# Turning the modulation rows of a two-block transformer in groups of four slabs instead of one by one

## The chip, the cores and the metric

The kernel runs on one core of a Trainium2 chip. The metric is the device time of one execution in microseconds (us). The engines are called as in the profile: PE is TensorE (PEld its weight loads), DVE is VectorE, ACT is ScalarE, POOL is GpSimd, SP is SyncE, which issues the weight transfers.

## What is computed

The whole program is two small networks, one after the other, on 256 tokens of width 1024. The change touches only the first one, a two-layer block that is steered by two condition vectors, `c` for the tokens of the picture and `c_ctx` for 256 context tokens. For each layer l:

```
m      = silu(c) @ w_mod[l] + b_mod[l]        # 1024 -> 6144, and the same for c_ctx
shift1, scale1, gate1, shift2, scale2, gate2 = split(m, 6)
h = h + gate1 * mixer(rmsnorm(h, norm1_g) * (1 + scale1) + shift1)
h = h + gate2 * ffn(rmsnorm(h, norm2_g) * (1 + scale2) + shift2)
```

The mixer is a projection `w_in` into eight blocks (pool, neighbourhood attention q/k/v, retention q/k/v and gate), then pooling, attention and retention, then `w_out`. All in fp32.

## The kernel before, in words

**Weights** come as a stream of slabs of up to 128 x 4096 fp32 (2 MB) through a ring of three slots. SP issues the two halves of slab n once slab n-3 has been used (`loads_sp`, L479). The order of the slabs is written out by hand in `slabs` (L173). The matrix `w_mod[l]` is cut into 12 slabs of 512 columns. Slabs 0 to 3 of layer 0 come first; slabs 4 to 11 come one behind each of the eight slabs of `w_in` of layer 0; the 12 slabs of layer 1 follow, and are used during attention (0 to 5) and retention (6 to 11) of layer 0.

**One modulation slab** takes four steps, on three engines:

1. `mod_pe` (L602): PE multiplies the slab by silu(c). The weights of the product are a 128 x 32 slice of `g.cs`, of which columns 0 and 1 hold silu(c) and silu(c_ctx) and the other 30 are zero. Eight chunks of 128 inputs are dealt over the four column groups of the array, two each, so the result is a 128 x 512 bank with two useful rows in each quarter (four partial sums).
2. `mod_act` (L634): ACT copies that bank into one of two buffers `mod_rows`.
3. `mod_sum_pe` (L620): four fp32 products of PE, each with 128 columns of `mod_rows` as weights and the first two columns of a 0/1 table as moving operand, turn the rows into columns and add the four partial sums.
4. `mod_dve` (L641): DVE adds the bias and writes 4 columns x 2 of `g.mod`; where a scale is complete, it also makes the gain (L656).

**Banks.** PSUM has eight banks. The rows of step 1 go to bank seven, in both layers. The result of step 3 goes to bank six in layer 0 and to bank seven in layer 1. So in layer 0 step 3 of slab i waits until DVE has read slab i-1, and in layer 1 step 1 of slab i+1 waits for step 4 of slab i. In layer 0 bank six also takes the attention's outputs.

**Order of the work.** Each engine's program is a list written by hand. At the start (`first_block`, L3297) PE does slab 0, its step 3, slab 1, the sum of squares of the first norm, step 3 of slab 1, then slabs 2 and 3 with their steps. In the projection (`proj_pe`, L1024) PE does, for each of the eight names, the products of `w_in`, then step 3 of the slab before, then step 1 of the next slab. ACT puts step 2 behind its copies of that name (`proj_act`, L1055), DVE puts step 4 two names later (`proj_dve`, L1089); for the name `pool` its step 4 stands behind the addition of the attention bias, L1202. In attention (`attn_mod_pe`, L1238) PE does step 1 at odd steps i and step 3 at the even step behind; DVE's step 4 is `attn_mod_dve` (L1248), in the same order; in the first four steps ACT also makes tables of powers for retention (`powers_act`, L1217). Retention (`ret_pe`, L1292) does step 1 at even i up to 10 and step 3 at i+1.

The weights of `w_in` and of `w_out` (layer 0) are split into two parts for three products in place of one (`upper_act` L521, `lower_dve` L531, `mm3` L466, with its products on L469, L470, L471). All plain fp32 products, those of the modulation among them, are on L475.

## Time and profile before

| | us |
|---|---|
| median of 3 runs | 2822.08 |
| lowest, highest | 2820.62, 2824.28 |
| span of the profiled execution | 2811.5 |
| PE busy in it | 2664.0 |
| modulation, from the first slab's product to the last slab's bias | 10.3 to 309.0 |

The execution's own time is not listed beside its profile; the span lies 10.6 us below the median, which is what lies around it. Rows give the start of an instruction in us from the start of the span, then its duration, the engine, line, operation and tiles, and in brackets how long the engine had been idle before it and what ended that. Consecutive instructions of one kind are one row ("x8"). The granted clock (PEclk) is 1.00 for TensorE's full clock and 0.50 for half of it.

### The profile page before, as it was taken

The page shows a single profiled execution, that of the slowest core. Times are in us where ns is not written, and L with a number is a line of the kernel's source. Part 1 is how long each engine was busy: PE and PEld are TensorE (multiplying, and loading weights), DVE is VectorE, ACT ScalarE, POOL GpSimd, SP SyncE. Part 2 cuts the span into 40 slices and gives each one's busy share as a digit, 9 for nine tenths or more (in the row PEclk, how much of TensorE's full clock was granted, in tenths as well). Part 3 has the DMA queues.
Part 4 walks back from the last instruction along what each step waited for, and adds up shares of the span by engine and source line. Part 5 has one row for each costly group of instructions (what it writes and reads, how often), then busy time and mean ns, then how long its engine had stood idle before and what let it go on. Part 6 is the DMA issues. An engine that isn't in the chain of part 4 may idle for free.

```text
span 2811.5 us, 38891 instructions
## 1 busy us (share of the span) xinstructions
PE 2664.0 (95%) x15416; PEld 2257.2 (80%) x15416; DVE 1820.9 (65%) x1912; ACT 1462.4 (52%) x1624; POOL 29.6 (1%) x40
## 2 busy tenths in 40 slices
PE   6999989999898999888899998899999999999998
PEld 4775678888786899777799986788888888888887
DVE  4224665543535776674355454688888889888887
ACT  3225343332325555522244444577777777777775
POOL 0002000000002000000000000000000000000000
PEclk9999999999999999998799999899999999999998
DMA  8456322222231445320044441699999999999996
GB/s 344 169 206 252 138 91 90 96 99 86 102 130 55 167 163 179 125 90 1 1 155 176 171 169 43 232 368 349 366 348 343 371 347 365 349 369 344 344 371 240
DMA packets 84359, 590.43 MB, mean 210 GB/s; under 512 B 9616, under 2 KB 10000, under 8 KB 19472
## 3 DMA queue, kind: packets, MB, share of 16 engines
q1 hardware_dynamic: 82800, 576.79, 55.0%
q10 hardware_dynamic: 1440, 11.93, 1.1%
q8 instruction: 90, 1.47, 0.2%
q14 instruction: 29, 0.24, 0.0%
HBM read 587.63 MB, written 1.05 MB: 209 GB/s over the span
## 4 chain that ended last, share of the span: by engine, by line
PE 85%; DVE 8%; ACT 4%; issue 1%; DMA 1%; DVEq 0%; POOL 0%; ACTq 0%; POOLq 0%; SPq 0%
PE banks L469 23%; PE banks L470 23%; PE banks L471 23%; PE banks L475 16%; DVE ring_rounded L531 2%; ACT ring_rounded L521 1%; PE banks L2869 1%; DMA ring<-in_stream 1%; PE banks L909 1%; DMA hT<-in_h 1%; DVE rstd L816 0%; DVE aT L2266 0%; ACT scratch L986 0%; DVE activations L1427 0%; DVE aT L832 0%
## 5 line engine op out<-in xcount | busy, mean ns | idle before, releaser
L531 DVE TENSOR_TENSOR ring_rounded<-ring,ring_rounded 128x2048 fp32r<-128x2048 f32 (+4 forms) x168 | 339.7, 2023 | 430.1 <-ACT ring_rounded L521 429.0
L470 PE MATMUL banks<-aT_rounded,ring_rounded 128*128 128x256 f32 (+1 forms) x1632 | 531.5, 326 | 0.0
L470 PE MATMUL banks<-ring_rounded,activations_rounded 128*128 128x512 f32 x1344 | 523.3, 389 | 0.0
L521 ACT ACTIVATE ring_rounded<-ring 128x2048 fp32r<-128x2048 f32 (+4 forms) x168 | 284.8, 1697 | 397.3 <-PE banks L471 381.7
L469 PE MATMUL banks<-aT_rounded,ring_rounded 128*128 128x256 f32 (+2 forms) x1120 | 339.0, 303 | 24.6 <-DVE aT_rounded L841 12.5
L470 PEld LDWEIGHTS banks<-aT_rounded,ring_rounded 128*128 128x128 f32 x1632 | 317.7, 195 | 23.8 <-issue 0.7
L471 PE MATMUL banks<-aT_rounded,ring_rounded 128*128 128x256 f32 (+2 forms) x1120 | 336.3, 300 | 0.0
L470 PEld LDWEIGHTS banks<-ring_rounded,activations_rounded 128*128 128x128 f32 x1344 | 252.7, 188 | 50.0
L3043 DVE TENSOR_TENSOR ring_rounded<-ring,aT_rounded 128x2048 fp32r<-128x2048 f32 x112 | 255.1, 2286 | 22.5 <-ACT aT_rounded L2961 21.5
L3043 DVE TENSOR_TENSOR ring_rounded<-ring,tables_rounded 128x2048 fp32r<-128x2048 f32 x112 | 254.0, 2286 | 23.5 <-ACT tables_rounded L2961 22.5
L2961 ACT ACTIVATE tables_rounded<-ring 128x2048 fp32r<-128x2048 f32 x112 | 215.0, 1920 | 85.2 <-DMA ring<-in_stream 75.3
L2961 ACT ACTIVATE aT_rounded<-ring 128x2048 fp32r<-128x2048 f32 x112 | 214.9, 1919 | 81.2 <-DMA ring<-in_stream 70.0
L469 PE MATMUL banks<-activations_rounded,ring_rounded 128*128 128x512 f32 (+1 forms) x724 | 246.6, 341 | 9.6 <-DVE aT_rounded L846 7.1
L469 PEld LDWEIGHTS banks<-aT_rounded,ring_rounded 128*128 128x128 f32 (+1 forms) x1120 | 218.7, 195 | 34.2 <-issue 18.8
L471 PE MATMUL banks<-activations_rounded,ring_rounded 128*128 128x512 f32 (+1 forms) x724 | 245.1, 339 | 0.0
L471 PEld LDWEIGHTS banks<-aT_rounded,ring_rounded 128*128 128x128 f32 (+1 forms) x1120 | 218.4, 195 | 5.7
L469 PE MATMUL banks<-tables_rounded,activations_rounded 128*128 128x512 f32 x448 | 176.5, 394 | 0.0
L469 PE MATMUL banks<-aT_rounded,activations_rounded 128*128 128x512 f32 x448 | 176.1, 393 | 0.0
L471 PE MATMUL banks<-tables_rounded,activations_rounded 128*128 128x512 f32 x448 | 174.7, 390 | 0.0
L471 PE MATMUL banks<-aT_rounded,activations_rounded 128*128 128x512 f32 x448 | 174.7, 390 | 0.0
L470 PE MATMUL banks<-activations_rounded,ring_rounded 128*128 128x256 f32 (+1 forms) x528 | 168.1, 318 | 0.0
L469 PEld LDWEIGHTS banks<-activations_rounded,ring_rounded 128*128 128x128 f32 x724 | 137.9, 190 | 26.4 <-issue 8.8
(333 smaller groups left out, 4774.3 us busy)
## 6 DMA issues: line engine op xcount, KB each, us to landing
ring<-in_stream SPq DMA_DIRECT2D x501, 1024.0 KB, 6.0
ring<-in_stream SPq DMA_DIRECT2D x32, 704.0 KB, 5.2
ring<-in_stream SPq DMA_DIRECT2D x28, 768.0 KB, 6.0
activations<-in_rpb ACTq DMA_DIRECT2D x2, 1536.0 KB, 6.2
ring<-in_stream SPq DMA_DIRECT2D x6, 512.0 KB, 5.0
tables<-in_tab_b ACTq DMA_DIRECT2D x1, 2436.0 KB, 8.8
tables<-in_tab_a ACTq DMA_DIRECT2D x1, 2304.0 KB, 13.0
hT<-in_h ACTq DMA_DIRECT2D x1, 2048.0 KB, 16.0
```

Of the source, the lines that this page charges most:

```text
L469: pe.matmul(out, exact(upper), exact(w_upper), start=start, stop=False)
L470: pe.matmul(out, exact(upper), exact(w_lower), start=False, stop=False)
L471: return pe.matmul(out, exact(lower), exact(w_upper), start=False, stop=stop)
L475: return pe.matmul(out, lhsT, rhs, start=start, stop=stop)
L521: act.activation(exact(upper), w, ACT.Copy).then_inc(g.s["act_pieces"], 1)
L531: dve.tensor_tensor(exact(w), w, rounded(upper), ALU.subtract).then_inc(g.s["dve_pieces"], 1)
L909: last = pe.transpose(ps[:, o * w + P * t:o * w + P * t + P], probs[:, j % 2, o, P * t:P * t + P], g.tab("ident"))
L2869: last = pe.transpose(g.psum[4 + q % 2][:, P * j:P * j + P], g.hb[:, q % 2, P * j:P * j + P], g.tab("ident"))
L2961: act.activation(exact(g.upper[u % UPPERS]), g.units[u % EXPERT_RING], ACT.Copy).then_inc(s["act_split"], 1)
L3043: dve.tensor_tensor(exact(w), w, rounded(g.upper[u % UPPERS]), ALU.subtract).then_inc(s["dve_split"], 1)
```

## The change

`MOD_GROUP = 4`. Four slabs share one bank: the silu(c) buffer becomes one row of 32 x 8 + 8 columns, in which the two columns of chunk k stand at 32 k + 6 and 32 k + 7. Slab j of a group takes as weights the 32 columns from 32 k + 2 (3 - j), so its two useful columns are 2j and 2j + 1 and the rest are zeros. The first product of the group starts the accumulation, the last ends it. Step 2, step 3 and step 4 come once for a group: one copy of ACT, four products of PE with eight moving columns instead of two, and two additions of DVE (one for each of the two condition vectors) on 16 columns.

```diff
+MOD_GROUP = 4
 def mod_pe(g, pe, l, i):
-    pe.wait_ge(*g.bank_free("seven"))
-    ps = g.open(("mod rows", l, i), "seven")
+    group, j = i // MOD_GROUP, i % MOD_GROUP
+    if j == 0:
+        pe.wait_ge(*g.bank_free("seven"))
+        g.open(("mod rows", l, group), "seven")
+    ps = g.psum[g.bank_of[("mod rows", l, group)]]
     for half in range(2):
         for c in range(4):
             k = 2 * c + half
-            last = mm(pe, ps[32 * c:32 * c + 32, :], g.cs[:, k, :], w[:, 512 * k:512 * k + 512], half == 0, half == 1)
+            first = 32 * k + 2 * (MOD_GROUP - 1 - j)
+            last = mm(pe, ps[32 * c:32 * c + 32, :], g.cs[:, first:first + 32], w[:, 512 * k:512 * k + 512],
+                      (j, half) == (0, 0), (j, half) == (MOD_GROUP - 1, 1))
 def mod_sum_pe(g, pe, l, group):
-    for j in range(4):
-        last = mm(pe, ps[:, 2 * j:2 * j + 2], g.mod_rows[:, i % 2, P * j:P * j + P], g.tab("mod_rows")[:, 0:2])
+    w = 2 * MOD_GROUP
+    for q in range(4):
+        last = mm(pe, ps[:, w * q:w * q + w], g.mod_rows[:, group % 2, P * q:P * q + P], g.tab("mod_rows")[:, 0:w])
 def mod_dve(g, dve, l, group):
+    for s in range(2):
+        out = g.mod[:, l, first:first + 4 * MOD_GROUP, s].rearrange("p (j q) -> p q j", j=MOD_GROUP)
+        b = g.vec[:, a:a + 4 * MOD_GROUP].rearrange("p (j q) -> p q j", j=MOD_GROUP)
+        dve.tensor_tensor(out, ps[:, :, :, s], b, ALU.add).then_inc(g.s["dve_modulation"], 1)
+def ends_group(i):
+    return i is not None and i % MOD_GROUP == MOD_GROUP - 1
 # proj_pe
-            if i > MOD_FIRST:
-                mod_sum_pe(g, pe, l, i - 1)
+            if i > MOD_FIRST and ends_group(i - 1):
+                mod_sum_pe(g, pe, l, i // MOD_GROUP - 1)
             mod_pe(g, pe, l, i)
 # attn_mod_dve
-    if l == 0 and i == 0:
-        mod_dve(g, dve, 0, 10)
     if l == 0 and i == 1:
-        mod_dve(g, dve, 0, 11)
+        mod_dve(g, dve, 0, 2)
 # first_block, ACT
+        squares_act(g, e, ("n1", 0), g.hT, T2, None)
         mod_act(g, e, 0, 0)
-        squares_act(g, e, ("n1", 0), g.hT, T2, None, then=lambda: mod_act(g, e, 0, 1))
-        for i in range(2, MOD_FIRST):
-            mod_act(g, e, 0, i)
 # first_block, PE
         mod_pe(g, e, 0, 0)
-        mod_sum_pe(g, e, 0, 0)
         mod_pe(g, e, 0, 1)
         for k in range(KD):
             sum_pe(g, e, ("n1", 0), T2, k)
-        mod_sum_pe(g, e, 0, 1)
         for i in range(2, MOD_FIRST):
             mod_pe(g, e, 0, i)
-            mod_sum_pe(g, e, 0, i)
+        mod_sum_pe(g, e, 0, 0)
```

The calls of steps 2, 3 and 4 in the projection, attention and retention are kept where a group ends and dropped elsewhere. Groups end with slabs 3, 7 and 11 of each layer: at the start, at the name `pool`, at `gate`, at attention step 7, and at retention steps 2 and 10; step 3 stands one place behind each of these (behind slab 3 at the start). DVE's first wait for the vectors stays, without its first addition.

## Rows read from the trace of the kernel before

**Rows 1.** The page: busy time by engine, share of the span, instructions.
```profile
PE 2664.0 (95%) x15416; PEld 2257.2 (80%) x15416; DVE 1820.9 (65%) x1912; ACT 1462.4 (52%) x1624; POOL 29.6 (1%) x40
```
**Rows 2.** Stretches of 20 us: length, busy by engine (instructions), PEclk, DMA share, GB/s.
```profile
100.00:120.00 20.00, 17.74 (x120) 14.35 (x119) 6.42 (x4) 5.09 (x8) 0.00 (x0) 0.83 0.66 258
...
200.00:220.00 20.00, 17.17 (x115) 10.44 (x112) 8.52 (x16) 15.09 (x34) 4.82 (x6) 0.83 0.61 240
...
260.00:280.00 20.00, 19.90 (x167) 10.74 (x166) 7.58 (x8) 8.44 (x16) 4.83 (x6) 1.00 0.83 306
280.00:300.00 20.00, 18.68 (x138) 9.05 (x137) 14.26 (x18) 9.30 (x13) 0.00 (x0) 1.00 0.77 292
```
**Rows 3.** PE's waits from 0 to 320 us: total, times, longest.
```profile
PE banks L475 <- DVE modulation L649: 5.8, 3, 2.3
...
PE banks L475 <- ACT scratch L999: 2.9, 3, 1.9
```
**Rows 4.** Line L637, step 2: duration ns min/median/max.
```profile
L637 ACT ACTIVATE mod_rows<-banks x24: 582/597/599, 14.0 to 301.8; 128x512 f32<-128x512 f32 x24
```
**Rows 5.** Timeline of PEld: step 3, then step 1, in the projection.
```profile
96.26 1.03 PEld L475 LDWEIGHTS banks<-tables,mod_rows 128*128 128x128 f32 x8
97.31 0.16 PEld L475 LDWEIGHTS banks<-ring,silu_c 128*32 128x32 f32 x8
...
99.16 0.19 PEld L469 LDWEIGHTS banks<-ring_rounded,scratch_rounded 128*128 128x128 f32 x1 [0.84 <-issue]
```
**Rows 6.** Timeline behind the products of `pool`.
```profile
112.87 0.17 DVE L649 TENSOR_TENSOR modulation<-banks,vectors 128x8 f32<-128x8 f32 x1
...
113.19 1.84 PE L475 MATMUL banks<-tables,mod_rows 128*128 128x2 f32 x8 [2.26 <-DVE modulation L649]
...
114.96 3.64 PE L475 MATMUL banks<-ring,silu_c 128*32 128x512 f32 x16
118.53 0.79 PE L469 MATMUL banks<-scratch_rounded,ring_rounded 128*128 128x512 f32 x1
...
119.87 0.39 PE L469 MATMUL banks<-scratch_rounded,ring_rounded 128*128 128x512 f32 x1
```
**Rows 7.** Line L489: second half of slab 3 with the one before, issue and landing.
```profile
L489 SPq DMA_DIRECT2D ring<-in_stream x2: 328/639/950, 14.0 to 14.4; - x2
...
DMA to landing us min/median/max: 13.4/14.4/15.5
```
**Rows 8.** Timeline of the start, slab 3.
```profile
31.43 1.92 PE L475 MATMUL banks<-ring,silu_c 128*32 128x512 f32 x16
...
33.42 0.60 ACT L637 ACTIVATE mod_rows<-banks 128x512 f32<-128x512 f32 x1 [3.03 <-PE banks L475]
...
35.16 0.17 DVE L649 TENSOR_TENSOR modulation<-banks,vectors 128x8 f32<-128x8 f32 x1 [3.46 <-PE banks L475]
```
**Rows 9.** Timeline of the first attention steps.
```profile
207.85 1.26 PE L475 MATMUL banks<-tables,mod_rows 128*128 128x2 f32 x8 [2.21 <-DVE modulation L649]
...
211.05 3.64 PE L475 MATMUL banks<-ring,silu_c 128*32 128x512 f32 x16
...
213.15 0.69 ACT L986 ACTIVATE scratch<-banks,nmax 128x512 f32<-128x512 f32 x1 [1.45 <-DVE nmax L952]
...
216.52 0.58 ACT L637 ACTIVATE mod_rows<-banks 128x512 f32<-128x512 f32 x1
...
221.48 1.01 ACT L999 ACTIVATE scratch<-banks 128x1024 f32<-128x1024 f32 x1
...
222.63 1.09 PE L475 MATMUL banks<-scratch,activations 128*64 128x128 f32 x16 [1.86 <-ACT scratch L999]
```
**Rows 10.** Timeline of the end of retention.
```profile
292.35 3.35 DVE L1427 RECIPROCAL activations<-activations 128x512 f32<-128x512 f32 x1 [1.56 <-ACT activations L1368]
...
298.63 1.92 PE L475 MATMUL banks<-ring,silu_c 128*32 128x512 f32 x16 [1.32 <-DVE modulation L649]
...
301.78 0.59 ACT L637 ACTIVATE mod_rows<-banks 128x512 f32<-128x512 f32 x1
...
302.51 1.02 PE L475 MATMUL banks<-tables,mod_rows 128*128 128x2 f32 x8 [0.90 <-ACT mod_rows L637]
```

More of the change, by code:

```diff
@@ L620, in mod_sum_pe @@
-def mod_sum_pe(g, pe, l, i):
-    if (l, i) == (0, 0):
+    if j == MOD_GROUP - 1:
+        g.also("pe_modulation", ("mm", "mod rows", l, group))
+def mod_sum_pe(g, pe, l, group):
+    if (l, group) == (0, 0):
         pe.wait_ge(g.const_in["tab_head"], 16)
-    pe.wait_ge(g.s["act_modulation"], g.at("free", ("mod rows", l, i)))
+    pe.wait_ge(g.s["act_modulation"], g.at("free", ("mod rows", l, group)))
     kind = "six" if l == 0 else "seven"
     pe.wait_ge(*g.bank_free(kind))
-    ps = g.open(("mod", l, i), kind)
-    for j in range(4):
-        last = mm(pe, ps[:, 2 * j:2 * j + 2], g.mod_rows[:, i % 2, P * j:P * j + P], g.tab("mod_rows")[:, 0:2])
+    ps = g.open(("mod", l, group), kind)
+    w = 2 * MOD_GROUP
+    for q in range(4):
+        last = mm(pe, ps[:, w * q:w * q + w], g.mod_rows[:, group % 2, P * q:P * q + P], g.tab("mod_rows")[:, 0:w])
@@ L630, in mod_sum_pe @@
     last.then_inc(g.s["pe_modulation"], 1)
-    g.count("pe_modulation", ("mm", "mod", l, i))
-def mod_act(g, act, l, i):
-    act.wait_ge(g.s["pe_modulation"], g.at("mm", "mod rows", l, i))
-    act.activation(g.mod_rows[:, i % 2, :], g.bank(("mod rows", l, i))[:, :], ACT.Copy).then_inc(g.s["act_modulation"], 1)
-    g.count("act_modulation", ("free", ("mod rows", l, i)))
-def mod_dve(g, dve, l, i):
-    if (l, i) == (0, 0):
-        dve.wait_ge(g.const_in["vec"], 16)
-    dve.wait_ge(g.s["pe_modulation"], g.at("mm", "mod", l, i))
-    a = g.vec_at["b_mod"] + 48 * l + 4 * i
-    ps = g.bank(("mod", l, i))[:, 0:8].rearrange("p (c s) -> p c s", s=2)
-    b = g.vec[:, a:a + 4].unsqueeze(2).broadcast_to((P, 4, 2))
-    dve.tensor_tensor(g.mod[:, l, 4 * i:4 * i + 4, :], ps, b, ALU.add).then_inc(g.s["dve_modulation"], 1)
-    g.count("dve_modulation", ("free", ("mod", l, i)))
+    g.count("pe_modulation", ("mm", "mod", l, group))
@@ new lines, in mod_act, with mod_dve @@
+def mod_act(g, act, l, group):
+    act.wait_ge(g.s["pe_modulation"], g.at("mm", "mod rows", l, group))
+    act.activation(g.mod_rows[:, group % 2, :], g.bank(("mod rows", l, group))[:, :], ACT.Copy).then_inc(g.s["act_modulation"], 1)
+    g.count("act_modulation", ("free", ("mod rows", l, group)))
+def mod_dve(g, dve, l, group):
+    dve.wait_ge(g.s["pe_modulation"], g.at("mm", "mod", l, group))
+    first = 4 * MOD_GROUP * group
+    a = g.vec_at["b_mod"] + 48 * l + first
+    ps = g.bank(("mod", l, group))[:, 0:8 * MOD_GROUP].rearrange("p (q j s) -> p q j s", q=4, j=MOD_GROUP)
+    for s in range(2):
+        out = g.mod[:, l, first:first + 4 * MOD_GROUP, s].rearrange("p (j q) -> p q j", j=MOD_GROUP)
+        b = g.vec[:, a:a + 4 * MOD_GROUP].rearrange("p (j q) -> p q j", j=MOD_GROUP)
+        dve.tensor_tensor(out, ps[:, :, :, s], b, ALU.add).then_inc(g.s["dve_modulation"], 1)
+        g.count("dve_modulation", ("free", ("mod", l, group)))
@@ L1344, in ret_pe @@
             mod_pe(g, pe, 1, mod_in_retention(i))
-        if l == 0 and i and mod_in_retention(i - 1) is not None:
-            mod_sum_pe(g, pe, 1, mod_in_retention(i - 1))
+        if l == 0 and i and ends_group(mod_in_retention(i - 1)):
+            mod_sum_pe(g, pe, 1, mod_in_retention(i - 1) // MOD_GROUP)
 def over_heads(g, pe, l, what, j):
@@ L1378, in ret_act @@
                 g.count("act_retention", ("free", ("ro", l, j)))
-        if l == 0 and mod_in_retention(i) is not None:
-            mod_act(g, act, 1, mod_in_retention(i))
+        if l == 0 and ends_group(mod_in_retention(i)):
+            mod_act(g, act, 1, mod_in_retention(i) // MOD_GROUP)
         if i == 0:
@@ L1445, in ret_dve @@
                 centre(j)
-        if l == 0 and i and mod_in_retention(i - 1) is not None:
-            mod_dve(g, dve, 1, mod_in_retention(i - 1))
+        if l == 0 and i and ends_group(mod_in_retention(i - 1)):
+            mod_dve(g, dve, 1, mod_in_retention(i - 1) // MOD_GROUP)
         if l == 0 and 5 <= i < 11:
@@ L3328, in first_block @@
         rstd_dve(g, e, ("n1", 0), T2)
-        for i in range(1, MOD_FIRST):
-            mod_dve(g, e, 0, i)
+        mod_dve(g, e, 0, 0)
     for l in range(2):
@@ L3426, in build @@
         g.pool_w = g.sb("pool_w", 2, 4, 64)
-        g.cs, g.mod, g.gain = g.sb("silu_c", KD, 32), g.sb("modulation", 2, 48, 2), g.sb("gain", 2, 2, KD, 2)
+        g.cs, g.mod, g.gain = g.sb("silu_c", 32 * KD + 2 * MOD_GROUP), g.sb("modulation", 2, 48, 2), g.sb("gain", 2, 2, KD, 2)
         g.cend = g.sb("chunk_ends", 4, 8)
```

34 lines of the change are left out of this document (17 added, 17 removed).

## Prediction

> **What bounds the kernel now.** I read the page first, for who is busy: PE is, 95% of the span [rows 1]. So a step taken off PE pays in full wherever PE is the one that others wait for, and a step taken off ACT or DVE pays only where PE waits for it. The modulation is over at 309 us, so I then read only the first 320 us, in stretches, for where PE is not full or not at its full clock. Between 100 and 120 us and between 200 and 220 us both are seen at once: busy 17.7 and 17.2 of 20 us, and a granted clock of 0.83 [rows 2]. The waits say why: PE waited 5.8 us in three waits for the modulation's bias addition on DVE [rows 3]. The timelines of these places give the rest.
>
> **Step 3, in the projection.** Its eight weight loads begin at 96.26 and those of the next slab at 97.31 [rows 5]; the loads before and behind run without a gap, so one step 3 costs PE 1.05 us at full clock. Eight moving columns instead of two lie behind these loads, and I cost them at nothing (bounds: nothing, and 0.3 us for each of the six, a quarter more). Step 1 itself, 97.31 to 99.16, is 1.85 us [rows 5] and keeps its number and shape. Between 60 and 195 us PE has one wait only, that of rows 6. Removed are steps 3 of slabs 4, 5, 6, 8, 9 and 10. Five of them at 1.05 are **5.3 us**; that of slab 6 is in the next part.
>
> **The wait behind `pool`.** Step 3 of slab 6 needs bank six, which DVE gives back at 113 us only, because its addition stands behind the attention bias. PE was idle 2.26 us, from 110.93 on. Then it ran at half clock: step 3 took 1.84, step 1 3.64 instead of 1.92, and the first products of the next slab come at 118.53; from 119.87 the product again takes its 0.39 [rows 6]. In the changed kernel nothing stands between the products of `pool` and slab 7: slab 7 is the last of its group and waits for no bank. Step 1 ends at 110.93 + 1.85 = 112.78, so the next products come 118.53 - 112.78 = 5.75 us earlier. The three products from 118.53 to 119.87 took 1.34 us and want 0.68. Together **6.3 us** (6.4, rounded down). What they need, the lower part of their slab, was ready before the bias addition began, so nothing else is late next.
>
> **The start.** PE loses three steps 3 and the waits for ACT's copies between slabs. But slab 3 cannot start before its second half is there: issued at 14.4 and 15.5 us to landing, 29.9 [rows 7]; it started at 31.43 [rows 8]. At full clock step 1, copy, step 3 and addition follow as before and all is 1.5 us earlier. But slab 2 now ends at about 27.5 (it starts when the squares are summed at 26, in place of 27.8), and 2.4 us of idle time open, as long as the two that were followed by half clock [rows 6, 9]. Then step 1 takes 3.64 less what ran before the fall and step 3 takes 0.8 more, about 1.9 us in all: 0.4 us later than before. A second addition on DVE is 0.1 us more. I take **0**, with -1 and +3 as bounds (the upper one if the clock also rises one step earlier in the first products).
>
> **The head of attention.** Step 3 of slab 11 waited 2.21 us for DVE's addition for slab 10, which stands behind the first maximum; then PE ran at half clock, step 1 again 3.64 [rows 9]. That wait goes: bank six was given back long before. But here PE is not what ends last. ACT makes exponentials and tables of powers in turn, 3.37 us a step (213.15 to 216.52), then a copy of rows 0.58, and PE waits for its copy of the first transposes, 221.48, with the next product at 222.63, 1.86 idle [rows 9]. Without PE's late second score product ACT would start its second step at 213.15 - 1.45 = 211.70, and without the copy two steps end at 211.70 + 2 x 3.37 = 218.44: 3.0 us earlier than 221.48. Against that stands the clock. In these 7.5 us PE then has only one score product and one transpose, about 2.2 us of work, and idles in gaps of 1 to 2 us. The two falls seen came after idle stretches of 2.26 and 2.21 us and the first lasted to 119.87, 6.7 us from 113.19 [rows 6, 9], so a fall is likely here and reaches into the work from 219 on, where PE is the bound. Its price is half of what lies in it, 2.6 of the 3.4 (half of 6.7) that a whole one costs. I take **0.4 us**; bounds -0.5 and 3.0.
>
> The Trainium skill (TensorE: Matmul & The Clock Gate, section HAM oscillation) says that products that come in bursts between waits make each burst start at the lower clock; it speaks against taking filler work off PE. By it this term is the 0.4, and the wait behind `pool` is worth what I gave it. The trace agrees at both waits, and shows no fall after gaps under 1.9 us.
>
> **The rest of attention.** Steps 3 of slabs 1, 2, 4 and 5 of layer 1 go (that of slab 0 lay in the head). PE is full here, at 1.0 us each: 3.9, less 0.2 where the next transpose waits for its exponentials instead. Two of the three waits for ACT's copy L999, 1.0 us together [rows 3], came because a copy of rows stood before it on ACT, 0.6 us each [rows 4]. Sum **4.7 us**, bounds 3 and 5.5.
>
> **Retention.** Here PE is 99% busy until 280 us [rows 2]. Steps 3 of slabs 6, 8 and 9 go, 3.0 us. That of slab 10 and the wait of 1.32 at 298.63 go too, but they save nothing: from 292.35 on DVE works through a reciprocal of 3.35 us and what follows, ACT through its own, and the last copy of rows comes from that chain at 301.78, with PE waiting for it [rows 10]. Its length doesn't change. In its place PE gets two idle stretches, 0.9 and 2.2 us, within about 4 us. If the clock falls there, the first products of `w_out`, where PE is the bound again, pay up to 3.4. I take 3.0 for it: **0 us** for retention, bounds -0.5 and 4.
>
> **At nothing**: the other copies of ACT and additions of DVE, which lie beside PE's work (ACT is busy 5 of 20 us in the projection [rows 2]); without that cover 18 x 0.6 us. SP is freed by the same instructions as before, and its transfers come as much earlier as PE does. In retention they fill 83% of the DMA engines [rows 2]; at 6 us a slab instead of 7 they would fill 97%, so no wait, but nothing to spare. The buffer of zeros is eight columns longer.
>
> **Sum.** 5.3 + 6.3 + 0 + 0.4 + 4.7 + 0 = 16.7 us. The span of 2811.5 becomes 2794.8; with the 10.6 that the median lies above it, 2805.4.
>
> **The rivals.**
> - *The clock holds.* The gaps that I price do not make it fall. Then the head of attention gives 3.0, retention 3.0, the start 1.5: 5.3 + 6.3 + 1.5 + 3.0 + 4.7 + 3.0 = 23.8, time 2798.3. For it: gaps of 0.7 to 1.9 us elsewhere were followed by full clock. Chance 0.17.
> - *Only the projection pays.* Attention's steps turn out to be set by the loop from score to exponential to transpose rather than by PE, and the gain there and in retention comes back as waits or as one more stretch at half clock. Then 11.6 less 1 to 2, time 2812. For it: ACT is 75% busy from 200 to 220 us [rows 2]. Against it: PE has few waits after 225. Chance 0.20.
> - *All but a remainder is given back* by stretches of half clock that fall elsewhere in the 2500 us behind, where nothing changes but the moment. Time 2820. Chance 0.07.
> - *Slower: the shifted slice.* Weights of step 1 now begin at columns that are not a multiple of 32. No row shows such a load. If it takes longer and is not hidden, it is paid in all 24 slabs, 16 loads each. It decides from 16.7 / 24 = 0.7 us a slab, 0.04 us on a load of 0.13 to 0.16 [rows 5]; at twice the load, 0.13 x 16 x 24 = 50, less 17, time 2855. Against it: the same number of columns, next to each other, as before. Chance 0.04.
>
> **The numbers.** The rest, 0.52, is the forecast, 2805.4. The range goes from the case in which the clock holds, with a little above it, to *only the projection pays* with 2 us more lost: 2797 to 2814. About 0.2% (5.6 us) is what a measurement of this kernel can tell from no change. Faster by more than that are the forecast, the first rival and nearly all of the second: 0.88; within it 0.08; slower 0.04.
>
> **What would show it.** Step 3 in six places instead of 24; PE's wait at 111 us gone and a granted clock of 1.00 from 100 to 120; PE at half clock around the first attention steps and at the first products of `w_out`, with the first transposed copy near 218 less what the projection saved (about 207). The timeline of slab 3: 29.9, and its duration says whether the clock fell. I am wrong if step 1 is longer than 1.92 at full clock, if new waits of PE for exponentials or transposed copies add up to more than 2 us, or if transfers of slabs end waits of PE in retention.

## The result and the profile after

The changed kernel takes 2838.14 us (median of 4, 2834.67 to 2840.51) beside 2821.35 for the kernel before (median of 4): ratio 1.0059, 95% interval 1.0038 to 1.0080. That is **slower** by 0.6%, little, but clear of the noise. The forecast was 2805.4 us, with a range of 2797 to 2814: wrong by 33 us and in sign.

The profiled execution took 2840.51 us with a span of 2838.7. The time is 1.8 us above the span here and in every other run. So the 10.6 us by which the median lay above the span of the kernel before are not what lies around an execution: its profiled execution was some 9 us faster than its median. The page's busy line for PE and its clock line, after:

```profile
PE 2697.7 (95%) x15272; PEld 2251.1 (79%) x15272; DVE 1817.3 (64%) x1900; ACT 1452.5 (51%) x1606; POOL 29.9 (1%) x40
...
PEclk9999999999999999988899996899999999999998
```

PE has 144 products fewer than before [rows 1] and is busy 34 us longer. So the loss is not waiting. The stretches by window tell where the time is. After, with the columns of [rows 2]:

```profile
100.00:120.00 20.00, 20.00 (x127) 16.37 (x126) 7.12 (x4) 6.27 (x8) 0.00 (x0) 1.00 0.71 281
...
280.00:300.00 20.00, 17.74 (x63) 13.58 (x64) 11.34 (x11) 4.98 (x7) 0.00 (x0) 0.83 0.32 129
...
1700.00:1752.00 52.00, 50.10 (x236) 29.33 (x237) 24.51 (x78) 22.97 (x88) 0.00 (x0) 0.51 0.00 1
1850.00:2290.00 440.00, 440.00 (x2032) 359.49 (x2031) 377.46 (x240) 321.52 (x224) 0.00 (x0) 1.00 0.95 349
```

The last two stretches of the kernel before:

```profile
1700.00:1752.00 52.00, 43.65 (x297) 29.12 (x296) 25.49 (x80) 25.73 (x91) 0.00 (x0) 0.93 0.01 3
1850.00:2290.00 440.00, 439.91 (x2076) 367.27 (x2075) 387.09 (x245) 327.89 (x226) 0.00 (x0) 1.00 0.96 357
```

From 1850 to 2290 us (the experts of the second network, which the change doesn't touch) PE is full and at full clock in both, yet does 2032 products instead of 2076, 2.1% fewer. And the second network's attention around 1700 to 1752 runs at half clock. Up to the end of the modulation the total is close to the forecast: the same addition of DVE stands at 310.04 before and at 294.13 after, 15.9 us earlier (forecast 16.7). The row after is shown with the end of retention below; before:

```profile
310.04 0.69 DVE L1420 SCALAR_TENSOR_TENSOR activations<-banks,activations 128x512 f32<-128x512 f32 x1 [1.10 <-PE banks L475]
```

The products of the experts, first and last of seven in a row on PE's timeline. Before:

```profile
1994.77 0.39 PE L471 MATMUL banks<-tables_rounded,activations_rounded 128*128 128x512 f32 x1
...
1996.13 0.39 PE L471 MATMUL banks<-tables_rounded,activations_rounded 128*128 128x512 f32 x1
```

After:

```profile
1994.73 0.40 PE L472 MATMUL banks<-aT_rounded,activations_rounded 128*128 128x512 f32 x1
...
1996.13 0.40 PE L472 MATMUL banks<-aT_rounded,activations_rounded 128*128 128x512 f32 x1
```

Six steps from start to start take 1.36 us before, 0.2267 each, and 1.40 after, 0.2333 each. In the page's largest group of them the mean went with it, from 389 to 396 ns. Before:

```profile
L470 PE MATMUL banks<-ring_rounded,activations_rounded 128*128 128x512 f32 x1344 | 523.3, 389 | 0.0
```

After:

```profile
L471 PE MATMUL banks<-ring_rounded,activations_rounded 128*128 128x512 f32 x1344 | 531.6, 396 | 0.0
```

Same instructions, same shapes, same clock. What differs is in the change's last small line: `silu_c` became eight columns longer, and every buffer allocated behind it, `activations` and `scratch` among them, begins 32 bytes later in each partition. `hT`, `aT`, `ring` and `tables`, allocated ahead of it, stay. The addresses in the two programs, in bytes in each partition: ring 49280, aT 32896, activations 150912, scratch 210816 before; activations 150944 and scratch 210848 after.

### The profile page after: what moved, and what is told of

Same layout as the page of the kernel before. It is cut to its first block, busy times and chain, and to the rows that moved or that the text cites. A ratio compares the mean times of both kernels' runs of the same rounds, so it can differ in the third digit from the quotient of the medians.

```text
span 2838.7 us, 38554 instructions
## 1 busy us (share of the span) xinstructions
PE 2697.7 (95%) x15272; PEld 2251.1 (79%) x15272; DVE 1817.3 (64%) x1900; ACT 1452.5 (51%) x1606; POOL 29.9 (1%) x40
## 3 DMA queue, kind: packets, MB, share of 16 engines
HBM read 587.63 MB, written 1.05 MB: 207 GB/s over the span
## 4 chain that ended last, share of the span: by engine, by line
PE 86%; DVE 7%; ACT 4%; issue 1%; DMA 1%; DVEq 0%; POOL 0%; SPq 0%; POOLq 0%; ACTq 0%
PE banks L470 23%; PE banks L471 23%; PE banks L472 23%; PE banks L476 15%; DVE ring_rounded L532 2%; DMA ring<-in_stream 1%; ACT ring_rounded L522 1%; PE banks L2882 1%; PE banks L924 1%; DVE rstd L831 0%; ACT scratch L1001 0%; DVE aT L2279 0%; DVE activations L1440 0%; DVE aT L847 0%; DVE scratch L2070 0%
## 5 line engine op out<-in xcount | busy, mean ns | idle before, releaser
L471 PE MATMUL banks<-ring_rounded,activations_rounded 128*128 128x512 f32 x1344 | 531.6, 396 | 0.0
L3056 DVE TENSOR_TENSOR ring_rounded<-ring,aT_rounded 128x2048 fp32r<-128x2048 f32 x112 | 253.4, 2284 | 10.8 <-ACT aT_rounded L2974 10.6
```

The source lines that it names most:

```text
L471: pe.matmul(out, exact(upper), exact(w_lower), start=False, stop=False)
L3056: dve.tensor_tensor(exact(w), w, rounded(g.upper[u % UPPERS]), ALU.subtract).then_inc(s["dve_split"], 1)
```

## The experiments

The question is whether that address is the cause, and by what rule. The table has, for every kernel, the ratio to the kernel before on the same chip with its interval, and from its profiled execution the length of four sections in us, each from one instruction of DVE to another that all kernels have: "feed-forward" (310 to 847 us of before: most of `w_out`, the first feed-forward and the projection of the second layer), the attention of the second network (1714 to 1737), and the two loops over the experts (1837 to 2299, and from there to the last of DVE's instructions). The ratio comes from several executions, the sections from one. The diffs below are shortened to the lines that matter; "..." and left-out ends of lines are unchanged code.

| kernel | ratio (95%) | feed-forward | attention 2 | experts 1 | experts 2 |
|---|---|---|---|---|---|
| before | 1 | 537.2 | 23.0 | 461.2 | 508.1 |
| the changed kernel | 1.0059 (1.0038 to 1.0080) | 544.2 | 33.7 | 471.4 | 518.4 |
| before_shifted | 1.0107 (1.0086 to 1.0129) | 544.2 | 33.7 | 471.4 | 517.3 |
| before_big_shifted | 1.0107 (1.0083 to 1.0131) | 544.4 | 33.7 | 472.0 | 517.6 |
| after_aligned | 1.0063 (1.0042 to 1.0084) | 548.9 | 23.0 | 470.9 | 517.0 |
| after_silu_last | 0.9937 (0.9915 to 0.9958) | 536.2 | 23.0 | 462.4 | 507.4 |
| after_in_place | 0.9938 (0.9921 to 0.9954) | 536.3 | 23.0 | 460.9 | 506.5 |
| before_stationary_shifted | 1.0071 (1.0054 to 1.0088) | 537.8 | 23.0 | 471.6 | 517.9 |
| before_scratch_shifted | 1.0011 (0.9990 to 1.0032) | 539.7 | 23.0 | 463.1 | 509.5 |
| before_bias_last | 0.9977 (0.9958 to 0.9995) | 538.3 | 23.0 | 461.5 | 508.7 |
| after_on_256 | 0.9941 (0.9924 to 0.9957) | 536.2 | 23.0 | 462.6 | 508.1 |
| before_attention_shifted | 1.0004 (0.9992 to 1.0016) | 537.8 | 23.0 | 463.0 | 509.2 |
| before_delta_shifted | 1.0001 (0.9991 to 1.0011) | 538.1 | 23.0 | 463.0 | 508.1 |
| before_delta_and_attention | 0.9993 (0.9982 to 1.0004) | 536.7 | 23.0 | 462.9 | 508.1 |
| before_first_block_shifted | 1.0047 (1.0021 to 1.0074) | 545.8 | 23.0 | 463.6 | 509.2 |
| before_big_experts_back | 1.0103 (1.0079 to 1.0126) | 545.9 | 23.0 | 470.3 | 516.2 |
| before_big_scratch_back | 1.0117 (1.0098 to 1.0136) | 546.0 | 24.2 | 472.9 | 517.8 |
| before_all_shifted | 0.9995 (0.9981 to 1.0010) | 538.0 | 23.0 | 462.6 | 509.4 |
| after_silu_first | 0.9942 (0.9927 to 0.9957) | 536.1 | 23.0 | 463.2 | 510.1 |
| before_stationary_128 | 1.0073 (1.0049 to 1.0097) | 536.8 | 23.0 | 472.6 | 518.5 |

**Is it the address?** *before_shifted* adds nothing to the kernel before but 32 unused bytes behind `silu_c`:

```diff
-g.cs, g.mod, g.gain = g.sb("silu_c", KD, 32), g.sb("modulation", ...
+g.cs, g.shift_pad, g.mod, g.gain = g.sb("silu_c", KD, 32), g.sb("shift_pad", 8), g.sb("modulation", ...
```

> The kernel before with eight unused fp32 columns (32 bytes) allocated behind silu_c, so that every buffer behind it (modulation, gain, rstd, activations, scratch) starts 32 bytes later, off a multiple of 64, as in the changed kernel. Nothing else differs. Theory A (the loss is the address): PE's 512-column products that read activations come every 0.230 us in place of 0.227, and the time rises by 25 to 45 us over the kernel before, to 2846 to 2866 us. Theory B (the loss is the new order of work, or the weights taken from shifted columns): no change, 2815 to 2825 us.

2853.22 us, 31 above before. No work was added, so the address alone costs that. *before_big_shifted* puts the 32 bytes directly ahead of `activations`, so that the small buffers stay:

```diff
+g.shift_pad = g.sb("shift_pad", 8)
 big = g.sb_both("activations", 14976)
```

> The kernel before with the 32 unused bytes directly ahead of activations: the small buffers (modulation, gain, rstd, nmax) stay where they were, activations and scratch move. Theory A, large operands: the same loss as with everything shifted, 2846 to 2866 us. If the small buffers carry part of it, this one is that much faster. Theory B: no change.

2853.89 us: the small buffers carry nothing of it.

**Can the changed kernel be freed of it?** In *after_aligned* `two_gains` (32 bytes) is allocated behind `silu_c`, which puts `activations` 64 bytes off; in *after_silu_last* `silu_c` itself is allocated last, which puts it at -1024; in *after_in_place* `rinv` goes last, which puts `activations` and `scratch` exactly where before has them:

```diff
# after_aligned
-g.cs, g.mod, ... = g.sb("silu_c", 32 * KD + 2 * MOD_GROUP), g.sb("modulation", ...
+g.cs, g.two_gains, g.mod = g.sb("silu_c", 32 * KD + 2 * MOD_GROUP), g.sb("two_gains", KD), g.sb("modulation", ...
# after_silu_last, behind scratch and two_gains
+g.cs = g.sb("silu_c", 32 * KD + 2 * MOD_GROUP)
# after_in_place, behind scratch and two_gains
+g.rinv = g.sb("rinv", 2, 2)
```

> The changed kernel with the 32-byte buffer two_gains allocated directly behind silu_c instead of last, so that activations and scratch start on a multiple of 64 bytes again, 64 bytes later than before the change. Same instructions. Theory A: products at 0.227 us again, time 2805 us (the 16 us won by the end of the modulation are kept), 2798 to 2812. Theory B: 2835 to 2841 us, as the changed kernel.

> The changed kernel with the silu_c buffer allocated last, so that activations and scratch start on a multiple of 64 bytes, 1024 bytes earlier than in the kernel before. Theory A: the same as with two_gains moved, 2798 to 2812 us. If only the exact place of before is good (a rival within A: a larger period than 64 bytes), this one and the last differ by more than 5 us. Theory B: 2835 to 2841 us.

> The changed kernel with the rinv buffer allocated last: activations, scratch and two_gains lie at the very addresses of the kernel before, while modulation, gain, chunk_ends, rstd, eps, nmax and rsum keep the 32 bytes of displacement. Theory A (the address of activations and scratch is the whole cause): 2804, between 2799 and 2809, as with silu_c last. Theory B (silu_c last gained because something else moved, or because all buffers moved by 1024 bytes, not because the displacement was gone): above 2825.

2840.11, 2803.93 and 2800.96 us. The first was a miss: 64 bytes off is no better than 32, only the attention section came back, and the total did not follow it. The other two beat both kernels and are 18.0 and 18.9 us below the kernel before, where the forecast had said 16.7. PE in the experts' window of *after_in_place*:

```profile
1850.00:2290.00 440.00, 440.00 (x2095) 368.16 (x2094) 385.98 (x252) 329.36 (x229) 0.00 (x0) 1.00 0.95 354
```

The 2095 products beside 2076 before are no gain of their own: this kernel is 12 us further on in the loop when the window opens. The section of the table is the fair comparison, 460.9 beside 461.2.

**Which operand?** In the experts the tiles `hT2` and `xg` in `activations` are what PE loads as weights, and the rounded weight slabs in `ring`, `aT`, `tables` and `scratch` move past them. *before_stationary_shifted* moves only the four expert tiles, inside `activations` (`sg` and `yb` with `hT2` and `xg`); *before_scratch_shifted* moves only `scratch`:

```diff
# before_stationary_shifted
-g.part(b, 3072, 2, KE, P)   g.part(b, 10240, 2, KD, P), g.part(b, 12288, 2, FC), b[:, 13312:14336]
+g.part(b, 3080, 2, KE, P)   g.part(b, 10248, 2, KD, P), g.part(b, 12296, 2, FC), b[:, 13320:14344]
# before_scratch_shifted
+g.shift_pad = g.sb("shift_pad", 8)
 tmp = g.sb_both("scratch", 4608)
```

> The kernel before, with the four expert tiles hT2, xg, sg and yb moved by 32 bytes inside activations; all else in place, the moving operands too. Theory A1 (the stationary operand, loaded as weights from activations, makes the expert products 0.2333 instead of 0.2267 us): experts 461 to about 471 in each of both loops, total 2840, between 2835 and 2846. Theory A2 (the moving operand or the outputs and copies carry it): 2818 to 2826, products at 0.2267.

> The kernel before, with 32 unused bytes between activations and scratch: scratch alone is displaced. It holds the moving halves of the first norm, the probabilities of attention and one of the six places of expert uppers. Theory A1 (stationary operands in activations carry nearly all of it): 2820 to 2829, the second attention's stretch at half clock, which hangs on a few hundred nanoseconds, possibly there and worth 11 of it. Theory A2 (moving operands carry it): 2835 or more.

2840.76 and 2825.20 us (the second not to be told from before). The experts' 20 us (10.4 and 9.8 in the two loops) come from the operand that is loaded as weights, displaced against the rest. The other way round, in the first feed-forward, the slabs are the stationary operand and `activations` is what moves, and there too the step from start to start grows. PE's timeline in *after_in_place*, first and last of seven:

```profile
499.78 0.39 PE L471 MATMUL banks<-aT_rounded,ring_rounded 128*128 128x512 f32 x1
...
501.14 0.39 PE L471 MATMUL banks<-aT_rounded,ring_rounded 128*128 128x512 f32 x1
```

In the changed kernel:

```profile
499.67 0.40 PE L470 MATMUL banks<-activations_rounded,ring_rounded 128*128 128x512 f32 x1
...
501.06 0.40 PE L470 MATMUL banks<-activations_rounded,ring_rounded 128*128 128x512 f32 x1
```

1.36 against 1.39 us for six. The section has 1895 such products; at 4 to 5 ns each that is about 8 us, an estimate, beside 7.0 measured (7.9 against *after_in_place*).

**Is more alignment better?** *after_on_256* puts `eps`, `two_gains`, `nmax` and `rsum` ahead of `hT`, and `silu_c`, `rinv` and `chunk_ends` last. `hT`, `aT`, `ring`, `activations` and `scratch` then begin at a multiple of 256, where in before each of them lies at an odd multiple of 128:

```diff
+g.eps, g.two_gains = g.sb("eps", 4), g.sb("two_gains", KD)
+g.nmax, g.rsum = g.sb("nmax", 2, 2), g.sb("rsum", 2, 2)
 g.hT, g.aT = g.sb("hT", KD, T2), g.sb_both("aT", KD, T2)
```

> The changed kernel with the small buffers reordered so that hT, aT, ring, activations and scratch all begin at multiples of 256 bytes (in the kernel before all of them begin at an odd multiple of 128) and the expert places in tables too. Theory P128 (a multiple of 128 is all that a product wants): products stay at 0.2267 us, experts at 461 in the first loop, time as after_in_place, 2797 to 2806. Rival P256 (the larger multiple wins again, as 128 does over 32 or 64): products below 0.2267 us and a time below 2790.

2802.19 us: nothing is won by it.

**The attention at half clock.** The profiled executions of three kernels displaced by 32 bytes showed it, those of no others. *before_attention_shifted*, *before_delta_shifted* and *before_delta_and_attention* move the tiles that the second network's attention and its delta stage keep in `activations`, one set, the other, and both; *before_first_block_shifted* moves all tiles of the first network, and *before_big_scratch_back* displaces `activations` but not `scratch`:

```diff
# before_attention_shifted (and the decay rows likewise)
-g.q2 = {n: g.part(b, 1024 * i, 4, L) ...
+g.q2 = {n: g.part(b, 8 + 1024 * i, 4, L) ...
# before_delta_shifted: prj, lat, tok ... y, each + 8
-g.lat = g.part(b, 3600, 4, L)
+g.lat = g.part(b, 3608, 4, L)
# before_first_block_shifted
-g.part = part
+g.part, big = part, big[:, 8:14976]
# before_big_scratch_back
+g.shift_pad = g.sb("shift_pad", 8)
-big = g.sb_both("activations", 14976)
+big = g.sb_both("activations", 14968)
```

> The kernel before, with the projected tiles of the second block (fq, fk, mq, mk, fv, mv and the decay rows, in activations) moved by 32 bytes; the experts' tiles and all else in place. In every kernel with activations displaced by 32 bytes the stretch from 1714 to 1737 us ran at half clock, 33.8 us instead of 23.0, and in no other. Theory (the displaced tiles of that attention make it so): half clock there again, total 2831, between 2828 and 2836. Rival (it hangs on what ran before, the displaced delta stage or the moment): attention at 23.0 us, total 2817 to 2825.

> The kernel before, with the tiles of the delta stage of the second block (prj, lat, tok, lnw to y) moved by 32 bytes inside activations; attention's projected tiles, the experts' and all else in place. Theory (the displaced delta stage brings the second block's attention to half clock): 33 us instead of 23.0 from 1714 to 1737, total 2830, between 2827 and 2835. Rival (it takes both, or something of the first block): 23.0 us there, total 2816 to 2825.

> The kernel before, with the tiles of the delta stage and the projected tiles of attention moved by 32 bytes, the experts' in place. Theory (both together are what brings that attention to half clock): 33 us instead of 23.0, total 2831, between 2828 and 2836. Rival (neither; the moment decides, which the first block's slower products move): 23.0 us there, total 2816 to 2825.

> The kernel before, with every tile of the first block in activations moved by 32 bytes; the second block's and scratch in place. Theory M (slower products with a displaced moving operand, about 0.231 instead of 0.2267 us over the first feed-forward, also move or disturb what follows until the second block's attention stays at half clock): 310 to 847 us 6 to 7 us longer, the attention 33.8 instead of 23.0 us, total 2838, between 2832 and 2842. Rival (only the products are slower): total 2822 to 2829, the attention at 23.0 us.

> The kernel with 32 unused bytes ahead of activations and activations 32 bytes shorter (the end of it is not used), so that scratch lies where it did. Theory (activations carry all, scratch nothing): 2852, between 2848 and 2857, the attention at 33.8 us. Rival (the half clock in that attention needs scratch displaced too): the attention at 23.0 us and the total 10 less, 2838 to 2845.

2819.41, 2821.07, 2817.97, 2831.10 and 2856.29 us. The first three can't be told from the kernel before, and none of the five profiled executions has the stretch of 33.7 us. The fourth has the slower feed-forward by itself (545.8); its median fell between the ranges of theory and rival. Its 10 executions lie between 2825 and 2850: four from 2844 on, at a mean clock of 0.955 to 0.957, beside 0.963 to 0.966 in the other six. The fifth was profiled in the shortest of its four executions, 2844.32 at a mean clock of 0.965; the other three took 2856.04 to 2858.27 at 0.958 or 0.959, and may well have had the stretch. So what brings PE to half clock there is not settled. The same kernel has it or not from one execution to the next, and a single trace can't clear a displaced tile of it.

**One part of the change alone.** *before_bias_last* keeps all 24 steps 3 and only puts DVE's addition ahead of the attention bias at `pool`:

```diff
-        if name == "pool":
-            bias_dve(g, dve, l)
         if l == 0 and IN_ORDER.index(name) >= 2:
             mod_dve(g, dve, l, MOD_FIRST - 2 + IN_ORDER.index(name))
+        if name == "pool":
+            bias_dve(g, dve, l)
```

> The kernel before, with DVE's addition for the slab issued ahead of the attention bias at pool instead of behind it. One part of the change alone: the wait at 111 us goes, step 3 stays. Theory (the wait of 2.26 us and the half clock behind it cost 6.3 less the one step 3 of 1.05): 5.3 us faster, total 2816.6, between 2815 and 2818.5, granted clock 1.00 from 100 to 120 us. Rival (the clock falls there for another reason, or the 5 us are lost again later): 2820 to 2823.

2815.64 us, 4.2 below before. Its stretch from 100 to 120:

```profile
100.00:120.00 20.00, 20.00 (x139) 17.23 (x139) 7.74 (x5) 4.88 (x7) 0.00 (x0) 1.00 0.76 301
```

Busy without a gap and at full clock, beside 17.74 and 0.83 [rows 2]: the wait and the half clock behind it go by two lines of order alone. By the interval the gain is 1.4 to 11.8 us, which holds the 5.3 but does not prove it. The timelines say it closer: from step 1 of slab 6 to step 1 of slab 8 PE takes 33.52 us (96.09 to 129.61) where before had 39.11 (97.31 to 136.42), 5.6 us less.

**Do the parts add?** *before_big_experts_back* displaces `activations` by 32 bytes and moves the expert tiles on by 96 more, so that they lie at a multiple of 128 again:

```diff
+g.shift_pad = g.sb("shift_pad", 8)
-g.part(b, 3072, 2, KE, P)   g.part(b, 10240, 2, KD, P)
+g.part(b, 3096, 2, KE, P)   g.part(b, 10264, 2, KD, P)
```

> The kernel with 32 unused bytes ahead of activations, with the four expert tiles moved on inside it by 96 bytes more, so that they lie at a multiple of 128 again. Theory (the parts add: experts 20, the rest 12 to 14): experts at 461 us in the first loop, the attention still at 33.8 us, total 2833, between 2829 and 2838. Rival (the experts' tiles are not a part by themselves): above 2845.

2850.35 us, as the rival had it: the experts stayed slow (470.3). That broke the rule that all expectations so far had assumed, a multiple of 128 for each operand. The tiles were now 128 bytes off their old place, and still wrong. The addresses left another rule: in the kernel before `ring`, `aT`, the expert places in `tables` and `scratch`, `xg` and `hT2` all agree modulo 256. Three kernels tell the two rules apart, two by moving both operands and one by moving one of them by 128:

```diff
# before_all_shifted
+g.shift_pad = g.sb("shift_pad", 8)
 g.hT, g.aT = g.sb("hT", KD, T2), g.sb_both("aT", KD, T2)
# after_silu_first
+g.cs = g.sb("silu_c", 32 * KD + 2 * MOD_GROUP)
 g.hT, g.aT = g.sb("hT", KD, T2), g.sb_both("aT", KD, T2)
# before_stationary_128
-g.part(b, 3072, 2, KE, P)   g.part(b, 10240, 2, KD, P)
+g.part(b, 3104, 2, KE, P)   g.part(b, 10272, 2, KD, P)
```

> The kernel before, with the 32 unused bytes ahead of the first buffer: hT, aT, ring, tables, activations and scratch all move by 32 bytes together. Theory R (a product of the experts is fast when its stationary and its moving operand agree in their address modulo 256 bytes, wherever they lie): products at 0.2267 us, experts at 461 in the first loop, total 2821, between 2815 and 2827. Theory L (each operand wants a multiple of 128 of its own): both operands are off, experts at 471 or more, total 2853 or more.

> The changed kernel with silu_c allocated first of all: activations and scratch lie 32 bytes off, where the changed kernel had them, but ring, aT, hT and tables are displaced by 1056 bytes, which is 32 modulo 256 too. Theory R (agreement modulo 256): 2803, between 2797 and 2808. Theory L (a multiple of 128 for each): 2838 or more.

> The kernel before, with the four expert tiles moved by 128 bytes where before_stationary_shifted moved them by 32; all else in place. Theory R (agreement modulo 256): experts at 471 in the first loop, as by 32, total 2840, between 2835 and 2845. Theory L (a multiple of 128): experts at 461, total 2816 to 2825.

2819.98, 2804.28 and 2839.84 us: theory R in all three. The group of 1344 products in *before_all_shifted*, where every operand is off a multiple of 128:

```profile
L470 PE MATMUL banks<-ring_rounded,activations_rounded 128*128 128x512 f32 x1344 | 523.2, 389 | 0.0
```

and in *before_stationary_128*, where every operand is on one:

```profile
L470 PE MATMUL banks<-ring_rounded,activations_rounded 128*128 128x512 f32 x1344 | 530.5, 395 | 0.0
```

So products of this form are slower when the buffers that they read do not agree in their address modulo 256 bytes. Differences of 32, 64 and 128 from that all cost 2 to 3% of the step; a further 256 costs nothing (the difference of `xg` and `ring` is an odd multiple of 256 in before and a multiple of 512 in *after_on_256*). Products of `ring` past `aT`, which no run moved against each other, step at 227.1 ns in all twenty traces. The changed kernel put `activations` and `scratch` out of step with `ring`, `aT` and `tables`.

The rule goes for a run of products and not for each by itself. From 614 to 712 us of the changed kernel two products of three read `aT` and `ring`, which agree, and the third reads `activations`. First and last of ten in a row, in the changed kernel:

```profile
613.82 0.39 PE L471 MATMUL banks<-activations_rounded,ring_rounded 128*128 128x512 f32 x1
...
615.90 0.40 PE L471 MATMUL banks<-activations_rounded,ring_rounded 128*128 128x512 f32 x1
```

In *after_in_place*:

```profile
613.79 0.39 PE L470 MATMUL banks<-aT_rounded,ring_rounded 128*128 128x512 f32 x1
...
615.83 0.39 PE L470 MATMUL banks<-aT_rounded,ring_rounded 128*128 128x512 f32 x1
```

Nine steps take 2.08 us against 2.04: one product in three is out of step, and the average step of all three is 231 ns and not 227. Likewise the experts' products of `scratch` with `xg` and `hT2`, displaced together by 32 bytes in the changed kernel, step at 232 ns there among products that read `ring`. Whether a product's own two operands collide, or one product's moving operand with the next one's weights, no run tells apart.

And it goes for 512 moving columns alone. The second network has products of 256 columns, `activations` past `ring`. First and last of 21 in a row, in the changed kernel, where the two disagree:

```profile
1059.81 0.28 PE L471 MATMUL banks<-activations_rounded,ring_rounded 128*128 128x256 f32 x1
...
1062.15 0.28 PE L470 MATMUL banks<-activations_rounded,ring_rounded 128*128 128x256 f32 x1
```

In *after_in_place*, where they agree:

```profile
1059.79 0.28 PE L470 MATMUL banks<-activations_rounded,ring_rounded 128*128 128x256 f32 x1
...
1062.19 0.28 PE L472 MATMUL banks<-activations_rounded,ring_rounded 128*128 128x256 f32 x1
```

Twenty steps take 2.34 us out of step and 2.40 in step: here agreement is 2% slower, not faster. No run moved these products by themselves.

## Why the prediction was wrong

**The step that failed** stands under *At nothing*: "The buffer of zeros is eight columns longer." It was read as memory that nobody touches, and not as an address that everybody behind it has. It was the largest term. Against *after_in_place* the profile of the changed kernel gives back 22.4 us in the experts (10.5 and 11.9), 7.9 in the feed-forward, of which 4.2 come back between 847 and 1112 us, 10.7 in the second network's attention and 3.2 in the 100 us behind it: 40.0 of the 41.0 by which the spans differ. By the ratios (1.0059 and 0.9938) it is 34 us; the two profiles are of the longest of four executions and of the shortest of four. The parts in the experts and the feed-forward are shown to be the longer steps of the products. The 13.9 in and behind the attention go with a stretch at half clock, and that the address causes it is not shown.

*The shifted slice*, the rival that was slower, named the same line of the change for the wrong reason. Step 1 takes 1.92 to 1.93 us a slab at full clock after as before, so a slice that begins off a multiple of 32 columns costs nothing that shows.

**The other steps**, from the timelines of the changed kernel. *The start* was worth 1.6 and not 0. Slab 3 begins at 29.74 with the landing, as forecast, and the first product of `w_in` comes at 38.28, where before had it at 39.85. After:

```profile
29.74 1.92 PE L476 MATMUL banks<-ring,silu_c 128*32 128x512 f32 x16 [1.94 <-DMA ring<-in_stream]
...
38.28 0.76 PE L470 MATMUL banks<-scratch_rounded,ring_rounded 128*128 128x512 f32 x1 [4.83 <-DVE aT_rounded L861]
```

Before:

```profile
39.85 0.77 PE L469 MATMUL banks<-scratch_rounded,ring_rounded 128*128 128x512 f32 x1 [4.73 <-DVE aT_rounded L846]
```

Step 1 took 1.92 there: the clock did not fall in the idle 1.94 us. That is the term that the first rival had right. In *after_in_place* the same slab stands behind a longer idle time, longer than the two behind which the kernel before ran at half clock, and its step 1 is at full clock too:

```profile
29.75 1.92 PE L476 MATMUL banks<-ring,silu_c 128*32 128x512 f32 x16 [2.33 <-DMA ring<-in_stream]
```

So the length of the wait, by which the prediction priced the fall, does not decide. Nor does a fall need such a wait. The prediction read only the first 320 us and found none after gaps under 1.9 us; further on in the same trace there are some. Before:

```profile
1355.00:1362.00 7.00, 4.53 (x89) 3.30 (x87) 3.20 (x8) 2.03 (x3) 0.00 (x0) 1.00 0.01 2
1362.00:1393.00 31.00, 28.81 (x204) 23.08 (x205) 8.91 (x15) 2.83 (x6) 0.00 (x0) 0.50 0.00 1
```

PE's longest wait in the first of these stretches is 0.98 us. It then ran at half clock for 31 us, 93% busy.

*The wait behind `pool`* is gone as forecast, and step 1 takes half the time of [rows 6]:

```profile
107.53 1.93 PE L476 MATMUL banks<-ring,silu_c 128*32 128x512 f32 x16
109.38 0.50 PE L470 MATMUL banks<-scratch_rounded,ring_rounded 128*128 128x512 f32 x1
```

The product is 9.15 us earlier than the one at 118.53 [rows 6]; the forecast for this place was 5.75 and two steps 3, 7.85, to which the 1.6 of the start come.

*The projection as a whole* was worth 9.1 and not 11.6. Behind its last products stands step 1 of slab 11. Before:

```profile
196.91 1.92 PE L475 MATMUL banks<-ring,silu_c 128*32 128x512 f32 x16
```

After:

```profile
186.21 1.92 PE L476 MATMUL banks<-ring,silu_c 128*32 128x512 f32 x16
```

In *after_in_place*:

```profile
184.97 1.92 PE L476 MATMUL banks<-ring,silu_c 128*32 128x512 f32 x16
```

196.91 less 186.21 is 10.7, of which 1.6 are the start's. The wait behind `pool` gave what was forecast: from step 1 of slab 6 to step 1 of slab 8 the kernel before takes 39.11 us (97.31 to 136.42) and the changed one 33.01 (94.16 to 127.17), 6.1 less beside 6.3. The other steps 3 were priced too high. From step 1 of slab 4 to step 1 of slab 5 it is 19.23 us before and 18.40 in *after_in_place*, and the other four places give the same: 0.8 us for a step 3 taken out, where the prediction read 1.05 between two weight loads. In the changed kernel it is 0.4 to 0.6, because the projection's products read `scratch`, and are slower too: *after_in_place* gains 10.4 here.

*The head of attention.* After:

```profile
194.87 1.06 PE L476 MATMUL banks<-tables,mod_rows 128*128 128x8 f32 x8
...
205.84 1.94 PE L924 MATMUL banks<-tables,scratch 128*128 128x128 f32 x8 [2.22 <-ACT scratch L1001]
...
207.60 1.02 ACT L1014 ACTIVATE scratch<-banks 128x1024 f32<-128x1024 f32 x1
...
208.76 1.98 PE L476 MATMUL banks<-scratch,activations 128*64 128x128 f32 x16 [0.99 <-ACT scratch L1014]
...
210.67 2.61 PE L476 MATMUL banks<-ring,silu_c 128*32 128x512 f32 x16
...
213.22 1.13 PE L476 MATMUL banks<-activations 64*128 64x256 f32 x8
```

The first transposed copy is at 207.60, forecast "about 207". The transposes of 1.94 and the product of 1.98 ran at half clock (1.09 each elsewhere), until within step 1 at 210.67: the fall came where it was forecast, with a wait of 2.22. That agrees with the Trainium skill (TensorE: Matmul & The Clock Gate, section HAM oscillation): products in bursts between waits start at the lower clock. The score product at 213.22 stood at 225.51 before, 12.3 earlier, against 10.7 at the end of the projection. So the head gained 1.6 where 0.4 was forecast (bounds -0.5 and 3.0).

*The rest of attention and retention* until the reciprocals: DVE's first one starts at 273.23, 19.1 before the 292.35 of [rows 10]. That is 6.8 us more, where 4.7 and 3.0 were forecast. The end:

```profile
282.66 0.58 ACT L646 ACTIVATE mod_rows<-banks 128x512 f32<-128x512 f32 x1
...
283.39 1.48 PE L476 MATMUL banks<-tables,mod_rows 128*128 128x8 f32 x8 [2.26 <-ACT mod_rows L646]
...
284.72 0.77 PE L470 MATMUL banks<-activations_rounded,ring_rounded 128*128 128x512 f32 x1
...
294.13 0.69 DVE L1433 SCALAR_TENSOR_TENSOR activations<-banks,activations 128x512 f32<-128x512 f32 x1 [4.07 <-PE banks L476]
```

The chain through the reciprocals does end in the last copy of rows, as forecast, with PE idle for 2.26 us, and the first products of `w_out` run at 0.63 us instead of 0.39 until 290.41. 19.1 shrinks to the 15.9 of DVE's addition at 294.13: 3.2 for a forecast of 3.0. The sum of it all is 1.6 + 9.1 + 1.6 + 6.8 - 3.2 = 15.9 beside 16.7. That they lie so close is in part luck: the start and the head gave 2.8 more than forecast, the projection and all that follows the head 3.6 less.

PE's waits from 0 to 320 us, after:

```profile
PE banks L476 <- DMA ring<-in_stream: 18.1, 3, 10.0
...
PE banks L924 <- ACT scratch L1001: 2.7, 2, 2.2
PE banks L476 <- ACT mod_rows L646: 2.3, 1, 2.3
...
PE banks L476 <- ACT scratch L1014: 1.4, 2, 1.0
PE banks L476 <- ACT scratch L1001: 1.2, 1, 1.2
```

DVE's additions for the modulation are gone from the list [rows 3]. One of the signs named for a wrong forecast came: PE waits 3.9 us for exponentials (L1001), 3.4 of it in the head of attention, where before had 0.4 (L986), and 1.4 for transposed copies (L1014) where before had 2.9. The new waits for exponentials, 3.5 us, are more than the 2 named. But nearly all of them lie in the head, where the forecast had reckoned with idle gaps of 1 to 2 us, and they did not bring the loss. The other signs stayed away: step 1 is 1.92, and no slab's transfer ends a wait in retention. The list had none for the 2500 us that the change doesn't touch, and there the forecast failed. The rival *all but a remainder is given back* had looked there, for clock alone.

## What to carry to other kernels

A buffer that grows moves all that is allocated behind it; put a buffer that changes size last, or compare the addresses of both versions before comparing times. In a kernel bound by rounded products of 512 columns, keep all the buffers that they read at addresses that agree modulo 256 bytes (not so for 256 columns here), and look at the step from start to start of one form of product in a stretch that the change doesn't touch: if that moved, the code isn't what changed the time.

## What the runs showed of the hardware

- A product of 128 x 128 by 512 columns in rounded fp32 takes a step of 0.2267 us at full clock when its operands agree modulo 256 bytes, and 0.231 to 0.233 when they differ by 32, 64 or 128. Products whose operands agree pay too when they stand between products whose operands don't (231 ns on average with one in three out of step). With 256 columns it is the other way round: 120 ns in step, 117 out of step by 32 bytes. Both operands may be off a multiple of 128 together at no cost (*before_all_shifted*). It holds for the stationary operand displaced against the moving one (experts) and the other way round (feed-forward). Why, no run here shows.
- The experts' weight loads themselves don't get longer in the profile (188 ns each before and after); it is the product's step that does.
- Long stretches at half clock come and go with the moment, also without a wait of PE over 1 us ahead of them (at 1362 us of before). A wait of 2.33 us was followed by full clock in *after_in_place*, waits of 2.21 and 2.26 by half clock in before. The section from 1292 to 1306 us took 13.6 us in the profiled execution of before and 22.6 to 23.4 in those of all other kernels, changed or not. A single trace therefore carries some 9 us of chance in this kernel, and the same part of the sum should be read from more than one.
